# Modulation chunks in bursts of four instead of one by one in two of the four up products of a two-layer decoder trunk

## The reference

```python
mods = (jax.nn.silu(c) @ ada_w + ada_b).reshape(B, 3, 3, 1, D_MODEL)     # shift, scale, gate of 3 sub-layers

def modulate(t, i):
    return t * (1.0 + mods[:, i, 1]) + mods[:, i, 0]
def residual(t, i, out, w):
    return _layer_norm(ALPHA * t + w * (1.0 + mods[:, i, 2]) * out, ln_g[i], ln_b[i])

x = residual(x, 0, _swiglu(modulate(x, 0), ffn_wg[0], ffn_wu[0], ffn_wd[0]), 0.5)
proj = modulate(x, 1) @ w_in
...
x = residual(x, 1, mix, 1.0)
x = residual(x, 2, _swiglu(modulate(x, 2), ffn_wg[1], ffn_wu[1], ffn_wd[1]), 0.5)
```

## Time and profile before

| what | value |
|---|---|
| median of 3 runs | 1797.05 us (1787.41 to 1798.69) |
| the profiled execution | 1793.23 us |
| its span | 1791.4 us |
| TensorE matmul (PE) | 1677.6 us busy, 94% |
| TensorE weight load (PEld) | 1528.4 us, 85% |
| VectorE (DVE) | 971.3 us, 54% |
| ScalarE (ACT) | 657.9 us, 37% |
| GpSimd (POOL) | 171.9 us, 10% |
| weights and states read | 261.83 MB, 150 GB/s over the span |

### The profile page before, as it was taken

How to read it: one execution, slowest core, us unless ns; L and a number is a source line. 1 busy time by engine, 2 the same in 40 slices (tenths; PEclk the granted TensorE clock), 3 DMA queues, 4 the chain that set the end, 5 groups by cost and what they waited for, 6 DMA issues and landing times.

```text
span 1791.4 us, 32978 instructions
## 1 busy us (share of the span) xinstructions
PE 1677.6 (94%) x14132; PEld 1528.4 (85%) x14132; DVE 971.3 (54%) x1640; ACT 657.9 (37%) x947; POOL 171.9 (10%) x217
## 2 busy tenths in 40 slices
PE   4999999989899899999989999999898989899997
PEld 2899998979668678999989999989877777799997
DVE  1444446584644676545465445466846457655544
ACT  2233334463221235433353333355522124543333
POOL 1000012100300131000120000110030013200011
PEclk9999999999895599999999999999999568999998
DMA  9455654434551054444636555643332203644441
GB/s 335 167 205 212 200 198 155 151 105 139 169 172 39 3 193 166 153 153 148 217 118 212 189 188 174 224 144 135 106 107 85 68 1 98 238 144 151 153 150 69
DMA packets 92370, 270.23 MB, mean 151 GB/s; under 512 B 27169, under 2 KB 29505, under 8 KB 91969
## 3 DMA queue, kind: packets, MB, share of 16 engines
q1 hardware_dynamic: 87808, 265.50, 43.2%
q10 hardware_dynamic: 4416, 2.62, 0.6%
HBM read 261.83 MB, written 6.26 MB: 150 GB/s over the span
## 4 chain that ended last, share of the span: by engine, by line
PE 81%; DVE 12%; ACT 3%; DMA 2%; issue 2%; POOL 1%; ACTq 0%; DVEq 0%; SPq 0%; POOLq 0%
PE psV L1904 12%; PE psV L1905 12%; PE psV L1906 12%; PE psA L1904 9%; PE psA L1905 9%; PE psA L1906 9%; PE psV L705 3%; DMA raw<-weights_dram 2%; PE psC L1919 2%; DVE wlo L2191 2%; DVE PJ L1419 1%; ACT whi L2066 1%; PE psY L1919 1%; DVE ZT L2232 1%; PE psV L694 1%
## 5 line engine op out<-in xcount | busy, mean ns | idle before, releaser
L2191 DVE TENSOR_TENSOR wlo<-raw,whi 128x1024 fp32r<-128x1024 f32 x340 | 421.2, 1243 | 440.4 <-ACT whi L2066 437.7
L2066 ACT ACTIVATE whi<-raw 128x1024 fp32r<-128x1024 f32 x340 | 358.5, 1056 | 327.0 <-PE psV L1906 322.6
L1904 PE MATMUL psA<-XH,whi 128*128 128x320 f32 x1200 | 383.8, 320 | 29.5 <-DVE XL L2243 18.9
L1905 PE MATMUL psA<-XL,whi 128*128 128x320 f32 x1200 | 375.6, 313 | 0.0
L1906 PE MATMUL psA<-XH,wlo 128*128 128x320 f32 x1200 | 375.2, 313 | 0.0
L1904 PEld LDWEIGHTS psA<-XH,whi 128*128 128x128 f32 x1200 | 229.5, 191 | 50.4 <-issue 30.6
L1904 PE MATMUL psV<-XH,whi 128*128 128x320 f32 x816 | 260.2, 319 | 7.4 <-DVE wlo L2191 7.2
L1905 PE MATMUL psV<-XL,whi 128*128 128x320 f32 x816 | 255.4, 313 | 0.0
L1906 PE MATMUL psV<-XH,wlo 128*128 128x320 f32 x816 | 255.1, 313 | 0.0
L1905 PEld LDWEIGHTS psA<-XL,whi 128*128 128x128 f32 x1200 | 229.8, 191 | 0.3
L1906 PEld LDWEIGHTS psA<-XH,wlo 128*128 128x128 f32 x1200 | 229.6, 191 | 0.0
(11 more groups left out here) (383 smaller groups left out, 1870.6 us busy)
## 6 DMA issues: line engine op xcount, KB each, us to landing
raw<-weights_dram SPq DMA_DIRECT2D x450, 512.0 KB, 3.4
raw_own<-weights_dram SPq DMA_DIRECT2D x30, 512.0 KB, 5.8
raw<-weights_dram SPq DMA_DIRECT2D x8, 256.0 KB, 3.7
ZS<-st_rw_dram SPq DMA_DIRECT2D x2, 768.0 KB, 4.4
S<-st_gla_dram ACTq DMA_DIRECT2D x2, 768.0 KB, 4.5
o_glas_dram<-S SPq DMA_DIRECT2D x2, 768.0 KB
o_rws_dram<-ZS SPq DMA_DIRECT2D x2, 768.0 KB
CON<-consts_dram SPq DMA_DIRECT2D x1, 1288.5 KB, 10.0
```

The source lines that it names most:

```text
L1904: mm(out, whi[:, n % SPL, k], hi[:, kt], start=first, stop=False)
L1905: mm(out, whi[:, n % SPL, k], lo[:, kt], start=False, stop=False)
L2066: activation(whi[:, n % SPL], buffer(DENSE[n]), ACT.Copy).then_inc(hi_done, 1)
L2191: tt(wlo[:, n % SPL], buffer(DENSE[n]), whi[:, n % SPL].bitcast(F32), ALU.subtract).then_inc(lo_done, 1)
```

## The change

In the first up of both layers the tiles are spread among bursts instead of single chunks: a burst is the four chunks of one group and then the fold of the group before it (none in the first burst); the last burst is only the last group's fold. What each chunk and fold computes, and the order among them, stay.

```diff
@@ -158,6 +158,13 @@
     return out + [("fold", *groups[-1])]
 
 
+def ada_bursts(groups):
+
+    bursts = [[("ada", *group, q) for q in range(4)] + [("fold", *g) for g in groups[max(n - 1, 0):n]]
+              for n, group in enumerate(groups)]
+    return bursts + [[("fold", *groups[-1])]]
+
+
 def two_groups(groups):
 
     return [("ada", *group, q) for group in groups for q in range(4)], [("fold", *group) for group in groups]
@@ -176,7 +183,8 @@
     def after(steps, left):
         return steps[:4] + list(left) + steps[4:]
 
-    out = after(spread([(step, int(k >= 2)) for k, step in enumerate(up[0])], ada_groups(in_ffn) if in_ffn else []), folds)
+    tiles = spread([([step], int(k >= 2)) for k, step in enumerate(up[0])], ada_bursts(in_ffn))
+    out = after([step for steps in tiles for step in steps], folds)
     steps, left = product(("down", L, 0), 0, in_gaps[0])
     out += steps
     rest = [("proj", L, t) for t in PROJ_ORDER[NRW:]]
```

## The result

The changed kernel takes 1860.06 us (median of 4 runs, 1857.16 to 1863.24), the kernel before 1792.99 us beside it; the ratio is 1.0374, interval 1.033 to 1.0419. It is slower by 67 us. The profiled execution took 1861.43 us (span 1859.6), 68.2 more than the profiled one before.

What follows compares the result with a forecast made beforehand. PE was taken to bound both first ups. Waits of 38.6 us and a slow clock of 18 us made 56.6 us on the profiled 1793.23 us, so 1850 us, with a range from 1826 to 1870.

Steps and rivals of the forecast that it cites:

- first part: In both layers' first ups PE is busy nearly throughout at full clock, so any wait there is paid in full.
- Part 1: On PE, a burst with all data ready takes 2.45 us instead of 3.65, 1.2 less.
- Part 2: q3, a burst's fourth chunk, waits for dense chunk n+3's split; lands T + 6.5, T being when the next tile could begin.
- The waits' price: PE's waits in the ten bursts: eight at 3.9 us, the layers' first at 3.3 and 4.1, 38.6 us together.
- Part 3: PE's waits lower TensorE's clock behind each burst: 1.8 us each, 18 us in all, bounds 0 and 2.6 each.
- The first chunk's place: Layer 0's first chunk lay in the 1.4 us wait for the split and cost nothing; its first burst adds 3.3 us.
- The clock did not stay up: Rival in both first ups: the waits come but the clock stays up, 1832 us; chance 0.16.
- Contention: Rival: loads behind the burst's last chunk take its bandwidth, landing takes 5.4 us, up to 1876 us; chance 0.12.
- The gain case: Rival: each burst's last chunk lands in time and mode changes are saved, -12.4 us, 1781 us; chance 0.06.

Runs made afterwards that it cites:

- e1: The changed kernel with the chunks of the two first ups in the six buffers raw_own: 1785.45 us, ratio 0.9959 to the kernel before.
- e3: The changed kernel with unread matmuls in PE's waits, 9 behind each burst's second chunk and 23 behind its third: 1833.54 us, ratio 1.0238.
- e9: The kernel of e1 once more, beside that of e10 and with more runs: 1781.71 us, ratio 0.9946.
- e4: The changed kernel with dense chunks loaded two ahead of a burst, not three: 1791.09 us, ratio 0.9998 to the kernel before.
- e6: As e3, but with only the 23 unread matmuls behind each burst's third chunk: 1835.7 us, ratio 1.0257.
- e10: The kernel before, single chunks, with those of the two first ups in raw_own, run again beside e9: 1790.25 us, ratio 1.000.
- e5: As e3, but with only the nine unread matmuls behind each burst's second chunk: 1857.95 us, ratio 1.0382.
- e8: The changed kernel with bursts of two chunks instead of four, in the four shared buffers: 1789.11 us, ratio 0.9984 to the kernel before.

## Why the prediction was right

The forecast was 1850 (1826 to 1870), by waits and a slow clock; 1860 was measured, by these. Step by step:

- **PE sets these stretches** (first part). Right: 66.6 of the 68.2 us lie in the two stretches.
- **What the burst saves** (Part 1: 2.45 us instead of 3.65). Right but for a small step: 2.5 us in e1. Part 1 took 0.37 us from a fold to its tile, as between tiles; behind a chunk it is 0.47 (e1, e3). Over ten bursts the estimate was 12.4 us; the medians gave 7.6 (e1) and 9.5 (e9), the traces 10.2 and 9.3 in the two first ups. Most of the rest is seen: e1's first burst still had a wait and took 1.2 us more than e9's, and in e9 the clock fell behind the empty wait at the start of layer 0, for 1.6 us.
- **q3 hangs on the split of n+3** (Part 2). Right, and shown both ways: another ring (e1) or one place in the order (e4) takes the loss away. The chain read T + 2.88 for the issue, as forecast. q3's load landed after 3.2 to 3.7 us, 3.5 in the mean, where I had taken 3.6; the lowest is under my bound of 3.3.
- **The waits' price** (38.6 us). Right: put the starts of q3 that the profile after shows into the same sum, with everything behind q3 at full speed (0.57, 0.47 and 0.10), and it gives 38.0. In the profile after the waits are 45.8 us of emptiness; forecast "some 50".
- **The clock** (Part 3: 1.8 us a burst, at most 2.6). This term was mis-sized: 2.55 us a burst, 25.5 in place of 18, just inside its upper bound. I priced only the matmuls of the tiles behind the wait. They lose 1.8 us, just as taken, but q3 and the fold run slow as well, 0.44 and 0.41 us more (1.01 and 0.88 against 0.57 and 0.47; the two bursts without a fold, only the 0.44): the clock falls in the wait, ahead of q3. The rows I took the price from had no work left between the wait and the tiles. That is 7.5 of the 11.6 us by which the measured 68.2 exceeds the 56.6 of the sum.
- **The first chunk's place** (Part 2: it "cost nothing"). The forecast counted it as no time saved, and nothing more. Moved away, it left a wait of 1.95 us empty, and the clock fell behind it in layer 0: 1.6 us that no term had. 38.0, 25.5 and 1.6 make 65.1 of the 66.6; the rest is not assigned.
- **The rivals.** The clock did not stay up. The profiled executions of e3 and e6 (1833.01 and 1832.84) come to the 1832 of that case in part by luck, as q3 comes later in them and the work outside the two first ups was shorter than in the kernel before (by 6 us in e3). Contention didn't come: no q3 took 5.4 us to land. The gain case was a fair price for a condition that the change doesn't meet. That e9's median, 1781.71, equals the forecast 1781 is luck: it lies 9.5 us under the kernel before beside it, not 12.4. The rule of the Trainium skill behind it (TensorEngine Tiling (Array Packing), Key Properties), that a change of the mode drains TensorE, is borne out by e9 against e10 as far as the cost goes, 8.5 us over ten bursts; that it is a drain no run shows. It is far less than one late buffer costs.
- **Slips in the range.** By its own terms the low end is 1824 (1832 less 3 for the landing and 5 for what is hidden), not 1826, and two thirds of the way to 1876 is 1867, not 1870. Nothing measured hangs on either.

## What to carry to other kernels

Before loads are put together that were spread, write down for each which earlier item must leave its buffer, and when that happens against the time of use: here a burst as long as the ring made its last load wait for a split that starts only when the burst is due. Short-lived data belong in buffers that nothing slow holds, or one place earlier in the order of loads. When a wait of TensorE is priced, everything behind it counts at the lower clock, the small matmuls inside the burst too. A gain of a few microseconds is read in the stretches that were changed: here the rest of the kernel differed by 12 us from one trace to another.

## What was not expected of the hardware

A wait of 1.3 us with small matmuls around it left the clock up in all bursts of e6; one of 3.1 us between full work brought it down (e5, 0.93 over the stretch). With both, the clock was down before q3's load had landed: the granted clock was 1.00 up to 102.5 us and 0.50 from 102.7, and the load landed at 103.23. q3's eight matmuls took 1.01 us instead of 0.57, and those of the tile then stood 0.27 us apart.

In between, the length of a wait did not decide. The empty wait of 1.94 or 1.95 us behind layer 0's first three tiles was followed by slow matmuls in four of nine traces (the changed kernel, e3, e4, e9), for some 1.6 us each time; the same wait in layer 1 in none of twelve. In e8 waits of 1.1 and 0.5 us around a single chunk were enough once. What parts these cases was not settled.

Matmuls whose result is thrown away, in the same waits, were worth 26 us between the medians (21 in the two first ups of the traces), though they didn't shorten a wait.
